# One core: the first four units share their first two K tiles, with split loads and fourteen matmuls of ones before them

## What is computed

```python
def rmsnorm(x, g):
    xf = x.astype(jnp.float32)
    xf = xf * lax.rsqrt(jnp.mean(xf * xf, axis=-1, keepdims=True) + EPS)
    return (xf * g.astype(jnp.float32)).astype(x.dtype)

h = rmsnorm(x, mix_norm[0])
qkv = h @ w_qkv          # (512, 1024) @ (1024, 1536)
...
bias = rel_bias.astype(jnp.float32)[jnp.asarray(t5_bucket(rel))]
```

## Time and profile before

| | |
|---|---|
| time, median of 3 runs | 1094.66 us (1093.75 to 1096.02) |
| the profiled execution | 1097.09 us, its span 1095.3 us |
| PE busy | 1072.5 us, 98% of the span |
| DVE, ACT, POOL busy | 69%, 45%, 11% |
| DMA moved | 121.10 MB, mean 111 GB/s |

### The profile page before, as it was taken

The page is one execution under the profiler, slowest core; times in us unless marked ns, Lnnn a source line. Parts: engine busy times, 40 slices in busy tenths (PEclk is TensorE's granted clock), DMA queues, the critical chain, the costliest instruction groups (busy, mean ns, idle before and its releaser), DMA issues.

```text
span 1095.3 us, 15616 instructions
## 1 busy us (share of the span) xinstructions
PE 1072.5 (98%) x5892; PEld 918.7 (84%) x5892; DVE 751.1 (69%) x1091; ACT 493.1 (45%) x763; POOL 116.6 (11%) x109
## 2 busy tenths in 40 slices
PE   6999999999999999999999999999999999999996
PEld 5888788888899888898788888888888899888896
DVE  5588667767776667787554556867676876667786
ACT  6366554434443334454752345454344433334452
POOL 3100030000100000113021221030000100000122
PEclk9999999999999999999999999999999999999998
DMA  6612032225732225641222211132226742225632
GB/s 193 163 59 77 1 135 97 96 96 182 193 105 100 99 96 173 161 126 67 94 77 89 84 40 58 63 110 96 96 96 183 198 123 88 98 97 170 148 105 89
DMA packets 43371, 121.10 MB, mean 111 GB/s; under 512 B 5202, under 2 KB 10098, under 8 KB 43316
## 3 DMA queue, kind: packets, MB, share of 16 engines
q1 hardware_dynamic: 34736, 106.45, 28.0%
q0 software_dynamic: 4608, 11.54, 6.3%
q10 hardware_dynamic: 3972, 2.38, 1.2%
HBM read 116.93 MB, written 2.88 MB: 109 GB/s over the span
## 4 chain that ended last, share of the span: by engine, by line
PE 92%; DVE 5%; ACT 2%; DMA 1%; issue 1%; SPq 0%; DVEq 0%; ACTq 0%
PE PS L465 68%; PE PS L523 18%; PE PS L636 1%; PE PS L654 1%; PE PS L644 1%; DMA X<-xT 1%; DVE XL L1316 1%; PE PS L774 1%; DVE X L1841 0%; PE PS L806 0%; PE PS L793 0%; DVE WL L1299 0%; DMA DRAW_W<-w_down 0%; PE PS L777 0%; PE PS L808 0%
## 5 line engine op out<-in xcount | busy, mean ns | idle before, releaser
L465 PE MATMUL PS<-XH,WH 128*128 128x512 f32 x992 | 393.0, 396 | 8.3 <-DVE XL L1316 8.2
L465 PE MATMUL PS<-XH,WL 128*128 128x512 f32 x992 | 387.6, 391 | 0.0
L465 PE MATMUL PS<-XL,WH 128*128 128x512 f32 x992 | 387.3, 390 | 0.0
L465 PEld LDWEIGHTS PS<-XH,WH 128*128 128x128 f32 x992 | 187.0, 188 | 49.8 <-issue 11.5
L465 PEld LDWEIGHTS PS<-XH,WL 128*128 128x128 f32 x992 | 186.9, 188 | 39.5
L465 PEld LDWEIGHTS PS<-XL,WH 128*128 128x128 f32 x992 | 187.2, 189 | 39.1 <-issue 1.0
L893 ACT CAST WH<-WRAW 128x1024 fp32r<-128x1024 f32 x137 | 142.6, 1044 | 164.9 <-DMA WRAW<-w_up 108.4
L1299 DVE TENSOR_TENSOR WL<-WRAW,WH 128x1024 fp32r<-128x1024 f32 x137 | 172.4, 1258 | 17.7 <-ACT WH L893 17.2
L1337 DVE TENSOR_TENSOR GS<-PS,R 128x512 f32<-128x512 f32 x44 | 30.4, 692 | 120.7 <-PE PS L465 120.7
L523 PE MATMUL PS<-AH,DH_Z 128*128 128x256 f32 x352 | 98.7, 280 | 1.0 <-DVE X L1428 0.7
L523 PE MATMUL PS<-AL,DH_Z 128*128 128x256 f32 x352 | 97.8, 278 | 0.0
(11 more groups left out here) (232 smaller groups left out, 1490.6 us busy)
## 6 DMA issues: line engine op xcount, KB each, us to landing
WRAW<-w_up SPq DMA_DIRECT2D x88, 512.0 KB, 3.2
WRAW<-w_bin SPq DMA_DIRECT2D x24, 512.0 KB, 3.2
DRAW_W<-w_down SPq DMA_DIRECT2D x24, 384.0 KB, 4.1
DRAW_W<-w_down SPq DMA_DIRECT2D x24, 320.0 KB, 3.2
WRAW<-w_qkv SPq DMA_DIRECT2D x11, 512.0 KB, 4.5
WSUM_Z<-w_down SPq DMA_DIRECT2D x12, 384.0 KB, 6.0
WSUM_Z<-w_down POOLq DMA_DIRECT2D x12, 384.0 KB, 5.2
WSUM_Z<-w_down SPq DMA_DIRECT2D x12, 320.0 KB, 4.5
```

Source lines behind the costliest of these rows:

```text
L465: last = mm(PS[:, bank], w[:, c:c + P], x[:, kb], start=start and n == 0 and w is wh and x is hi, stop=stop and n == len(kbs) - 1 and w is wl)
```

## The change

It does five things, all in the first 25 us. The first 256 columns of the weights are loaded as a piece of their own for all four slots (SLOTS = 4) and queued right behind X[0]; unit 0's goes on ACT's queue, ahead of GAIN. The remaining 768 columns of units 0 to 3 are queued later, unit 0's between X[2:4] and X[4:6], the others behind x. PE first multiplies K tile 0 for units 0 to 3, each into its own bank, then K tile 1, and then finishes unit after unit; the mean square stands inside unit 2 behind its K tile 4. Fourteen matmuls of ones, 128 x 128 by 128 columns into bank 7, stand ahead of it all on PE. ACT and DVE make the pieces in the matching order; the copy of TB now stands behind square 6 (before: behind square 5), and hi_unit(4) and lo_unit(4) now come before the root and the reciprocal.

```diff
+WARMING = 14
...
+            def load_first(u):
+                sp.dma_start(WRAW[u][:, 0:FIRST], w_qkv[u, :, 0:FIRST]).then_inc(first_landed[u], 16)
+            def load_rest(u):
+                sp.dma_start(WRAW[u][:, FIRST:D], w_qkv[u, :, FIRST:D]).then_inc(raw_landed[u], 16)
             sp.dma_start(X[:, 0], xT[:, 0]).then_inc(x_landed[0], 16)
+            for u in range(1, SLOTS):
+                load_first(u)
             sp.dma_start(X[:, 1], xT[:, 1]).then_inc(x_landed[1], 16)
-            sp.dma_start(WRAW[0][:, FIRST:D], w_qkv[0, :, FIRST:D]).then_inc(raw_landed[0], 16)
             sp.dma_start(X[:, 2:4], xT[:, 2:4]).then_inc(x_landed[2], 16)
+            load_rest(0)
             sp.dma_start(X[:, 4:6], xT[:, 4:6]).then_inc(x_landed[3], 16)
             sp.dma_start(X[:, 6:8], xT[:, 6:8]).then_inc(x_landed[4], 16)
-            for u in range(1, A_O):
+            for u in range(1, SLOTS):
+                load_rest(u)
+            for u in range(SLOTS, A_O):
                 load(u, w_qkv[u])
...
+            pe.wait_ge(ones_set, 1)
+            for n in range(WARMING):
+                mm(PS[:, B7, 0:P], STD[:, 0:P], STD[:, 0:P], start=True, stop=True)
+            early = FIRST // P
+            for kb in range(early):
+                for u in range(SLOTS):
+                    pe.wait_ge(first_lo, u + 1)
+                    product(u, u, XH, XL, range(kb, kb + 1), kb, start=kb == 0, stop=False, part_ready=(xl_ready, 0))
+            rest(0, range(early, 8), part_ready=(xl_ready, 0)).then_inc(unit_done, 1)
             pe.wait_ge(rel_landed, 32)
             mm(PS[0:A_HEADS, B5, 0:REL], RB[0:32, :], HOT[0:32, :], start=True, stop=True).then_inc(tb_done, 1)
-            unit(1, 1, XH, XL)
+            rest(1, range(early, 8)).then_inc(unit_done, 1)
+            rest(2, range(early, 5), stop=False)
             pe.wait_ge(onesr_ready, 1)
             mean_square(0)
+            rest(2, range(5, 8)).then_inc(unit_done, 1)
+            rest(3, range(early, 8)).then_inc(unit_done, 1)
...
+            act.dma_start(WRAW[0][:, 0:FIRST], w_qkv[0, :, 0:FIRST]).then_inc(first_landed[0], 16)
             act.dma_start(GAIN[:], gains).then_inc(gain_landed, 16)
...
+            first_part(0)
+            act.wait_ge(gain_landed, 16)
+            first_x(0)
+            for u in range(1, SLOTS):
+                first_part(u)
+            for m in range(1, 4):
+                first_x(m)
+            x_square(0, 0)
+            rest_part(0)
+            first_x(4)
+            first_x(5)
+            x_square(0, 1)
+            first_x(6)
+            first_x(7)
+            rest_part(1)
+            x_square(0, 2)
+            x_square(0, 3)
+            rest_part(2)
+            x_square(0, 4)
+            x_square(0, 5)
+            rest_part(3)
+            x_square(0, 6)
+            act.wait_ge(tb_done, 1)
+            nc.scalar.copy(TB[0:A_HEADS, :], PS[0:A_HEADS, B5, 0:REL]).then_inc(tb_ready, 1)
...
+            x_square(0, 7)
+            hi_unit(4)
             std(0)
-            hi_unit(4)
             hi_unit(5)
...
+            first_part(0)
+            dve.wait_ge(gain_landed, 16)
+            first_x(0)
+            for u in range(1, SLOTS):
+                first_part(u)
+            for m in range(1, 4):
+                first_x(m)
+            rest_part(0)
+            for m in range(4, KT_D):
+                first_x(m)
+            rest_part(1)
+            add_square(3)
+            rest_part(2)
+            add_square(4)
+            add_square(5)
+            rest_part(3)
+            add_square(6)
+            add_square(7)
+            lo_unit(4)
             inverse_rms(0)
```

More of the change, by code:

```diff
@@ L250, in trunk @@
         unit_evac = sem("unit_evac")
-        first_landed, first_hi, first_lo = sem("first_landed"), sem("first_hi"), sem("first_lo")
+        first_landed = [sem(f"first_landed{u}") for u in range(SLOTS)]
+        first_hi, first_lo = sem("first_hi"), sem("first_lo")
         x_landed = [sem(f"x_landed{i}") for i in range(5)]
@@ L402, in load_chunk @@
                     load(next_unit + 3, src[3])
-            sp.dma_start(WRAW[0][:, 0:FIRST], w_qkv[0, :, 0:FIRST]).then_inc(first_landed, 16)
+            def load_first(u):
+                sp.dma_start(WRAW[u][:, 0:FIRST], w_qkv[u, :, 0:FIRST]).then_inc(first_landed[u], 16)
+            def load_rest(u):
+                sp.dma_start(WRAW[u][:, FIRST:D], w_qkv[u, :, FIRST:D]).then_inc(raw_landed[u], 16)
             sp.dma_start(X[:, 0], xT[:, 0]).then_inc(x_landed[0], 16)
+            for u in range(1, SLOTS):
+                load_first(u)
             sp.dma_start(X[:, 1], xT[:, 1]).then_inc(x_landed[1], 16)
-            sp.dma_start(WRAW[0][:, FIRST:D], w_qkv[0, :, FIRST:D]).then_inc(raw_landed[0], 16)
             sp.dma_start(X[:, 2:4], xT[:, 2:4]).then_inc(x_landed[2], 16)
+            load_rest(0)
             sp.dma_start(X[:, 4:6], xT[:, 4:6]).then_inc(x_landed[3], 16)
             sp.dma_start(X[:, 6:8], xT[:, 6:8]).then_inc(x_landed[4], 16)
-            for u in range(1, A_O):
+            for u in range(1, SLOTS):
+                load_rest(u)
+            for u in range(SLOTS, A_O):
                 load(u, w_qkv[u])
@@ L589, in down_phase, with rest @@
                 w12(n + 3)
[L592 to L596, removed]
+            def rest(u, kbs, **kw):
+                pe.wait_ge(lo_ready, u + 1)
+                return product(u, u, XH, XL, kbs, kbs[0], start=False, **kw)
+            pe.wait_ge(ones_set, 1)
[7 more added lines that the diff above has]
+            rest(0, range(early, 8), part_ready=(xl_ready, 0)).then_inc(unit_done, 1)
             pe.wait_ge(rel_landed, 32)
             mm(PS[0:A_HEADS, B5, 0:REL], RB[0:32, :], HOT[0:32, :], start=True, stop=True).then_inc(tb_done, 1)
-            unit(1, 1, XH, XL)
-            pe.wait_ge(lo_ready, 3)
-            product(2, 2, XH, XL, range(0, 4), 0, stop=False)
+            rest(1, range(early, 8)).then_inc(unit_done, 1)
+            rest(2, range(early, 5), stop=False)
             pe.wait_ge(onesr_ready, 1)
             mean_square(0)
-            product(2, 2, XH, XL, range(4, 8), 4, start=False).then_inc(unit_done, 1)
-            unit(3, 3, XH, XL)
+            rest(2, range(5, 8)).then_inc(unit_done, 1)
+            rest(3, range(early, 8)).then_inc(unit_done, 1)
             unit(4, 0, XH, XL)
@@ L1067, in _, with first_part, rest_part, first_x @@
             nc.scalar.copy(ONESR[:], STD[:, 0:P]).then_inc(onesr_ready, 1)
[L1068 to L1071, removed]
+            def first_part(u):
+                act.wait_ge(first_landed[u], 16)
+                nc.scalar.copy(WH[u][:, 0:FIRST], WRAW[u][:, 0:FIRST]).then_inc(first_hi, 1)
+            def rest_part(u):
+                act.wait_ge(raw_landed[u], 16)
+                nc.scalar.copy(WH[u][:, FIRST:D], WRAW[u][:, FIRST:D]).then_inc(hi_ready, 1)
+            def first_x(m):
                 if m in LANDED:
@@ L1074, in _ @@
                 x_hi(0, m)
[L1075 to L1094, removed]
+            first_part(0)
[22 more added lines that the diff above has]
+            nc.scalar.copy(TB[0:A_HEADS, :], PS[0:A_HEADS, B5, 0:REL]).then_inc(tb_ready, 1)
+            act.wait_ge(tb_ready, 1)
+            act.dma_start(bias_rows.rearrange("h (q r) -> h q r", q=64),
+                          TB[0:A_HEADS, :].rearrange("h (o r) -> h o r", o=1).to_broadcast([A_HEADS, 64, REL]))\
+               .then_inc(rows_out, 16)
+            x_square(0, 7)
+            hi_unit(4)
             std(0)
-            hi_unit(4)
             hi_unit(5)
@@ L1596, in ffn, with first_part, rest_part, first_x @@
                     lo_unit(B_V + 2)
[L1598 to L1602, removed]
+            def first_part(u):
+                dve.wait_ge(first_hi, u + 1)
+                c = slice(0, FIRST)
+                tt(WL[u][:, c], WRAW[u][:, c], WH[u][:, c].bitcast(F32), ALU.subtract).then_inc(first_lo, 1)
+            def rest_part(u):
+                dve.wait_ge(hi_ready, u + 1)
+                c = slice(FIRST, D)
+                tt(WL[u][:, c], WRAW[u][:, c], WH[u][:, c].bitcast(F32), ALU.subtract).then_inc(lo_ready, 1)
+            def first_x(m):
                 if m in LANDED:
@@ L1605, in _, with add_square @@
                 x_lo(0, m)
[L1606 to L1612, removed]
+            def add_square(m):
                 dve.wait_ge(sq_ready, m + 1)
@@ L1615, in _ @@
                 tt(SS[:], SS[:], SQ[:, m % 2], ALU.add).then_inc(ss_ready, 1)
-            lo_unit(3)
+            first_part(0)
[17 more added lines that the diff above has]
+            lo_unit(4)
             inverse_rms(0)
@@ L1625, in _ @@
                 last.then_inc(unit_evac, 1)
-                if t:
-                    lo_unit(4)
             for t in range(2):
```

## The result

The changed kernel takes 1098.63 us (1097.25 to 1100.47, 7 runs), the kernel before 1094.66 (1092.88 to 1096.02, 7 runs beside them): a ratio of 1.0034 [1.0025, 1.0043], slower by 2.7 to 4.7 us. The forecast was 1095.5, the range ended at 1098.2. The profiled execution of the changed kernel took 1098.64 us, its median; that of the kernel before lay 2.4 above its own median, so the two spans (1096.7 and 1095.3) are closer together than the kernels are. What the change does is read from its own stretch, not from the spans.

The account below looks back on a forecast made before the run. PE, busy 98% of the span, was taken as the bound. Its 3.0 us lead is lost waiting for constants, which land at 42.0 against 41.23: median 1094.66 + 0.8 = 1095.5 us, range 1091.2 to 1098.2.

Parts of the forecast that it names:

- the one on the clock: PE idles 3.8 us before the transposes; the clock was taken to stay at its upper level, adding nothing.
- likeliest case: The forecast itself: constants late before the transposes, clock kept high, +0.8 us, 1095.5 us; chance 0.50.
- rival 2: Clock falls in PE's idle time before the transposes: +2.8 to +4.0 us, 1097.5 to 1098.7; chance 0.18.
- The price of the fall: Transposes and unit 5 start slow: 10 to 16 slow matmuls at 0.2 us each, 2.0 to 3.2 us.
- Constants late: Before the transposes: bias_rows issued 1.7 us later, so constants land at 42.0 against 41.23, +0.8 us.
- The slack in the kernel before: Time by which the constants landed before PE reached them at 41.23: between 0 and 1.3 us, 0.9 taken.
- load(5) stands behind bias_rows: load(5), issued at 23.5 on SP's queue, waits until bias_rows is through and lands over 8 us later.
- rival 1: load(5) gets through beside bias_rows, landing before 28 us, and PE's lead lives: 1091.7 against the median; chance 0.22.
- POOL holds DVE: In the start, POOL's add of square 2 goes first; DVE's rest of WL[1] ends only at 19.1.
- PE's lead: PE starts unit 4 at 32.45 against 35.48, 3.0 us ahead, and ends it at 38.2.
- Warming: Fourteen matmuls of ones before data arrives cost at most 0.2 us; PE then runs at 0.23 us a matmul.
- rival 3: Warming at the start does nothing: no change in the forecast, up to 2 us back in rival 1; no chance given.

Follow-up runs that it names:

- e5: The changed kernel without the fourteen matmuls of ones: 1098.63 us, ratio 1.0029 to the kernel before.
- e8: The changed kernel with the DMA of bias_rows moved behind hi_unit(5) on ACT's queue: 1099.83 us, ratio 1.0038 to the kernel before.
- e1: The filling kernel: the changed kernel with 18 more matmuls of ones behind unit 4, before the wait for the constants: 1096.31 us, ratio 1.0011.
- e10: The changed kernel with ACT's hi_unit(5) moved behind the fourteen DMAs of constants: 1092.99 us, ratio 0.9984 to the kernel before.
- e9: e2 with the rest of WH[2] cast ahead of squares 2 and 3 on ACT: 1091.03 us, ratio 0.9965 to the kernel before.
- e11: The same kernel as e2, timed again: 1091.47 us, ratio 0.9964 to the kernel before.
- e2: The changed kernel with the fourteen DMAs of constants on SP's queue, ahead of load(4): 1092.15 us, ratio 0.9979 to the kernel before.
- e6: The changed kernel with the constants on SP's queue and without the matmuls of ones: 1092.38 us, ratio 0.9965 to the kernel before.
- e3: The kernel before with the constants issued by SP behind load(3): 1095.31 us, ratio 0.9997 to the kernel before.
- e4: The kernel before with fourteen matmuls of ones ahead of the first real one: 1094.82 us, ratio 0.9998 to the kernel before.
- e7: The kernel before with the matmuls of ones and the constants on SP's queue, old start order: 1094.44 us, ratio 0.9988.

## Why the prediction missed, step by step

**The step that failed is the one on the clock.** The prediction saw the gap (3.8 us of idle PE in front of the transposes), called it the longest after the start, priced a fall of the clock within it, and then kept the clock high in its likeliest case, because "it is short beside the work around it". That was an opinion: no row spoke for it. The measured gap is 4.26 us and the clock fell, as it did behind the gaps of 4.5 and 5.2 us in e5 and e8; the page (TensorE: Matmul & The Clock Gate, section "Why this matters for your kernels") of the Trainium skill, which warns of exactly this, was named beside the rival, and the rival was given 0.18. Here trace and page agree, with 3.25 us for fourteen transposes that took 1.53. The forecast with the fall in it, rival 2, was 1097.5 to 1098.7; measured, 1098.63. The mechanism and its price were on paper; the likeliest case put that term at nothing, and it was 2.3 us. The range was also cut at 1098.2, inside that rival's own interval, and so missed by 0.4.

**The price of the fall** was given as 10 to 16 slow matmuls, 2.0 to 3.2 us. The trace has 1.72 us more for the transposes and 0.79 for the matmuls behind, 2.5 together. Of this 0.2 us comes behind any gap: from the first transpose to the scores it is 9.71 us in the earlier trace rows, 9.94 in e1 and 9.92 in e10, where the clock stayed, and 12.22 in the changed kernel. So the fall costs 2.3 us by the trace (1.8 in e8), and the filling kernel gave back 2.3.

**Constants late: right in kind, wrong in its parts.** bias_rows was to be issued 1.7 us later, at 22.3; it was 21.43, 0.84 later. ACT's chain ran as worked out, but each of its small waits was shorter: XH started at 9.22 instead of 9.5, and POOL's add of square 2 ended at 17.64 instead of 18.3, so that square 4 began at 17.68 instead of 18.9. The last constant was issued only 0.26 us later (38.66 against 38.40). The slack in the kernel before was read about rightly. The trace's record of the constants' semaphore has its last update at 40.14 (40.3 was taken), 0.3 us behind the end of the bytes in the earlier trace rows, and PE loads the first weights for the transposes at 40.83, without a wait. The changed kernel's load of the same weights stands below it:

```profile
40.83 1.69 PEld L616 LDWEIGHTS PS<-IDENT,VT 128*128 128x128 f32 x14
41.65 2.85 PEld L636 LDWEIGHTS PS<-IDENT,VT 128*128 128x128 f32 x14 [4.68 <-DMA GARAW<-w_ga]
```

What the sum did not have is the time that the last constant is under way: 1.74 us before (38.40 to 40.14), 2.95 in the changed kernel (38.66 to 41.61). A load on SP's queue goes with it. load(8) is issued when unit 4 is done. In the changed kernel that is at 37.43, ahead of the last constant, and it lands at 41.03; before, only load(7) is under way there, down at 39.04, and load(8) comes at 41.26, behind the constants. So PE's own lead seems to put a load in front of the constants that PE then waits for; no run tests this by itself. The constants came 1.47 us later (1.7 forecast), from other parts than forecast, so that this is close is luck. Against a slack of 1.1 (41.23 less 40.14) it makes +0.4 us at the transposes in this pair of traces; +1.2 by the filling kernel's time, +0.8 forecast.

**load(5) stands behind bias_rows: right.** Issued at 22.92 (forecast 23.5), landed 9.65 us later (forecast over 8). e8 shows the cause. The Trainium skill (DMA: Bandwidth & Descriptors, section "Issuing engines are not separate DMA queues") has it that DMAs of different issuing engines interleave; here a load of 512 KB waited some 6.5 us on such a neighbour. The measurement decides, and rival 1, which would follow from that sentence, did not happen.

**POOL holds DVE: right.** POOL's add of square 2 and the rest of WL[1] ran into each other:

```profile
16.19 1.45 POOL L1930 TENSOR_TENSOR SS<-SS,SQ 128x512 f32<-128x512 f32 x1 [0.91 <-ACT SQ L933]
...
16.41 2.04 DVE L1642 TENSOR_TENSOR WL<-WRAW,WH 128x768 fp32r<-128x768 f32 x1
```

2.04 us instead of 0.96, ended at 18.45; 19.1 was forecast, and "before 18.2" would have been wrong. e9 took the collision away, and the operation took 0.94.

**PE's lead: right, a little too small.** Stalls of 0.2 and 0.5 us (0.9 and 0.8 forecast; by its own numbers, 13.3 less 12.5, the first is 0.8), unit 1 done at 22.9 (23.3), the mean square at 24.8 (25.4 to 26.3 with its matmuls), unit 4 done at 37.4 (38.2). The lead of 3.0 us in the prediction came out as 3.8 at the end of unit 4 here (41.23 less 37.4); once nothing stands in the way it is 3.5 at the scores in e11 and 2.4 in e2, where x landed 1 us later. It widened the gap, from the 3.8 expected to 4.26.

**Warming: right.** It is free, the first real matmul is fast, and it changes nothing in this kernel (e5). The up to 2 us that rival 3 gave it where PE's lead lives were not found either (e6).

**What stays open.** At the scores the changed kernel is 2.94 us late in this pair of traces; by the ratio it is slower by 3.7 (2.7 to 4.7). The rest is within what varies from execution to execution. A part of that is when x lands: unit 4 of the old start began at 35.48 in the earlier trace rows but at 33.97 in e3, where the XH of X[2:4] started at 8.61 instead of 9.41. Another part arises far behind the change. Compared matmul by matmul, the changed kernel's trace is 2.7 us behind that of the kernel before up to 868 us, 0.8 behind at 998, and 1.8 at the end. A stretch of the kernel before, then of the changed one:

```profile
870.00:880.00 10.00, 10.00 (x88) 9.84 (x87) 9.19 (x14) 5.08 (x7) 1.75 (x2) 1.00 0.57 143
```

```profile
870.00:880.00 10.00, 10.00 (x91) 10.00 (x90) 9.46 (x14) 4.83 (x6) 0.88 (x1) 1.00 0.75 205
```

88 matmuls in 10 us against 91, with PE busy throughout and the same granted clock. What sets this was not tried.

## What to carry to other kernels

An engine made faster ahead of an unchanged wait gains nothing and stands idle longer; on PE, the idle gap of 4.3 us here cost another 2.3 us behind it, because the clock fell. A faster engine also releases its next loads sooner, and these may go ahead of what it waits for. So find the last of the waits that stand behind the saving, and what its transfer is queued behind, before speeding up the start; here moving one call (hi_unit(5)) was worth 5.6 us, more than the restructuring gives at its best (3.8 in e11). Where a rival's mechanism is written down and no row speaks against it, its interval belongs in the range whole.

## What the runs showed of the hardware

**When the clock falls.** Gaps of PE in mid-work, and the rate behind them: 4.3, 4.5 and 5.2 us (the changed kernel, e5, e8), slow each time; 2.68 (e4, with 0.61 us of idle time shortly before it), slow; 2.63 (e7), fast; 1.1 (e10), 0.3 (e1), fast.

**One DMA that holds all queues.** bias_rows moves from 16 partitions to DRAM in 1024 pieces and takes nearly 10 us. Behind it a load of the other queue took 9.65 us instead of 3.1, and on its own queue three small issues stood 3.36 to 3.95 us (e8, e10), where those of the changed kernel take 0.30 to 0.57. ACT, which issues them, started nothing else meanwhile.

**A small DMA's landing.** The last constant (64 KB) landed 1.74 and 1.81 us behind its issue in the kernel before and in e4, and 2.8 to 3.1 us in the changed kernel, e1, e5, e8 and e10. In the first two a 512 KB load of the other queue had landed within 0.7 us of that issue, in the others it took another 1.6 to 2.4 us.
